# Folding three quarters of the squared channels on VectorE before TensorE's sum for a norm

## What is computed

```python
def rmsnorm(x, g):
    xf = x.astype(jnp.float32)
    var = jnp.mean(xf * xf, axis=-1, keepdims=True)
    return (xf * lax.rsqrt(var + RMS_EPS)).astype(x.dtype) * g

for i in range(DEPTH):                      # first block
    xn = rmsnorm(h, norm_g[i])
    ...
    h = h + jnp.concatenate([y_hg, y_nsa], axis=-1) @ w_out[i]
    gate = jax.nn.sigmoid(rmsnorm(h, ple_norm_g[i]) @ w_pg[i])
    h = h + gate * (p[i] @ w_pp[i])
```

## Time and profile before

| | |
|---|---|
| median of 3 runs | 1159.08 us (1154.74 to 1159.19) |
| the profiled execution | 1159.57 us, its span 1157.7 us |
| TensorE's mean granted clock in it | 0.958 of full speed |
| busy: TensorE, VectorE, ScalarE, GpSimd | 1070.8, 692.2, 583.0, 5.0 us |
| TensorE's weight loads | 1006.8 us |
| read from HBM | 161.43 MB, mean 140 GB/s |
| chain that ended last | TensorE 76%, VectorE 10%, ScalarE 8%, DMA 2% of the span |

### The profile page before, as it was taken

One profiled execution on the slowest core, in us unless ns is written; L12 is line 12 of the kernel. 1 busy time (PEld: TensorE's weight loads), 2 busy tenths in 40 slices (PEclk: granted clock), 3 DMA queues, 4 the chain that ended last, 5 costly groups with the idle time before them and its releaser, 6 DMA issues.

```text
span 1157.7 us, 21354 instructions
## 1 busy us (share of the span) xinstructions
PE 1070.8 (92%) x9033; PEld 1006.8 (87%) x9033; DVE 692.2 (60%) x1020; ACT 583.0 (50%) x830; POOL 5.0 (0%) x13
## 2 busy tenths in 40 slices
PE   3999887898999898999999999999899899999997
PEld 3998776898996776899998999999879789999996
DVE  5556546565547355577665766666544557676664
ACT  4543565466435454565745545545444546545543
POOL 1000000000000000000000000000000000000000
PEclk8999889999999889999999999999998899999998
DMA  8543522253645221274454555555354235555531
GB/s 269 165 130 107 160 74 73 74 166 125 185 116 182 74 74 37 74 254 136 146 166 134 193 182 181 181 183 172 94 173 134 75 109 183 183 181 181 181 109 37
DMA packets 144746, 163.57 MB, mean 141 GB/s; under 512 B 6072, under 2 KB 135552, under 8 KB 144672
## 3 DMA queue, kind: packets, MB, share of 16 engines
q1 hardware_dynamic: 143752, 161.04, 43.3%
q10 hardware_dynamic: 632, 1.30, 0.3%
q0 software_dynamic: 288, 0.14, 0.0%
HBM read 161.43 MB, written 1.05 MB: 140 GB/s over the span
## 4 chain that ended last, share of the span: by engine, by line
PE 76%; DVE 10%; ACT 8%; issue 3%; DMA 2%; SPq 1%; DVEq 0%; ACTq 0%
PE ps L427 23%; PE ps L428 22%; PE ps L429 22%; ACT panels_high L1138 2%; DVE panels_low L1617 2%; PE ps L507 2%; ACT probs L1124 2%; PE ps L443 2%; DMA panels<-in_w_in 1%; DVE neg_max L1640 1%; DVE probs L1656 1%; PE ps L637 1%; PE ps L1031 1%; DMA q_nope<-in_ffn_conv_b 1%; DVE gate_o L2110 1%
## 5 line engine op out<-in xcount | busy, mean ns | idle before, releaser
L427 PE MATMUL ps<-input_high,panels_low 128*128 128x256 f32 x1792 | 525.3, 293 | 36.5 <-DVE input_low L1597 14.2
L428 PE MATMUL ps<-input_low,panels_high 128*128 128x256 f32 x1792 | 516.5, 288 | 0.0
L429 PE MATMUL ps<-input_high,panels_high 128*128 128x256 f32 x1792 | 516.3, 288 | 0.0
L1617 DVE TENSOR_TENSOR panels_low<-panels,panels_high 128x2048 fp32r<-128x2048 f32 (+1 forms) x146 | 330.3, 2265 | 290.7 <-ACT panels_high L1138 283.5
L427 PEld LDWEIGHTS ps<-input_high,panels_low 128*128 128x128 f32 x1792 | 353.6, 197 | 43.8 <-issue 24.9
L428 PEld LDWEIGHTS ps<-input_low,panels_high 128*128 128x128 f32 x1792 | 353.9, 197 | 0.8 <-issue 0.5
L429 PEld LDWEIGHTS ps<-input_high,panels_high 128*128 128x128 f32 x1792 | 353.5, 197 | 0.0
L1138 ACT CAST panels_high<-panels 128x2048 fp32r<-128x2048 f32 (+1 forms) x146 | 274.7, 1883 | 150.8 <-PE ps L429 131.0
L427 PE MATMUL ps<-ffn_hidden_high,panels_low 128*128 128x256 f32 x352 | 100.7, 286 | 3.8 <-DVE ffn_hidden_low L2124 3.8
L428 PE MATMUL ps<-ffn_hidden_low,panels_high 128*128 128x256 f32 x352 | 101.0, 287 | 0.0
L429 PE MATMUL ps<-ffn_hidden_high,panels_high 128*128 128x256 f32 x352 | 100.8, 286 | 0.0
(11 more groups left out here) (274 smaller groups left out, 1065.3 us busy)
## 6 DMA issues: line engine op xcount, KB each, us to landing
panels<-in_ffn_up SPq DMA_DIRECT2D x44, 1024.0 KB, 5.1
panels<-in_w_in SPq DMA_DIRECT2D x32, 1024.0 KB, 5.7
panels<-in_ffn_down SPq DMA_DIRECT2D x22, 1024.0 KB, 5.0
panels<-in_mix_w_in SPq DMA_DIRECT2D x20, 1024.0 KB, 5.3
panels<-in_w_out SPq DMA_DIRECT2D x8, 1024.0 KB, 5.3
panels<-in_w_pg SPq DMA_DIRECT2D x8, 1024.0 KB, 5.2
panels<-in_mix_w_out SPq DMA_DIRECT2D x8, 1024.0 KB, 6.6
panels<-in_w_pp SPq DMA_DIRECT2D x2, 1024.0 KB, 4.9
```

The lines of the kernel that those rows point to most:

```text
L427: pe.matmul(dst, w[1], x[0], start=start, stop=False if not kw else True, **kw)
L428: pe.matmul(dst, w[0], x[1], start=False, stop=False if not kw else True, **kw)
L429: return pe.matmul(dst, w[0], x[0], start=False, stop=stop, **kw)
L1617: V.tensor_tensor(low_slots[slot][:, 0:size], raw[n % SLOTS][:, 0:size], high_slots[slot][:, 0:size].bitcast(F32), ALU.subtract).then_inc( ...
```

## The change

For every norm but the first, VectorE adds squares elementwise in `SQ`, and TensorE sums fewer chunks. For norms 1, 3, 5, 6, 7 and 8, quarters 1 and 2 are added onto quarter 0 (`fold`), so that TensorE sums chunks 0 and 1, where quarter 2 was summed, and chunks 6 and 7: four sums in place of eight. For norms 2 and 4 (`pair_folds`) quarter 1 alone is added onto quarter 0: six sums in place of eight, the first two where quarter 1 was summed. A new semaphore, `sq_folded`, counts the finished folds, and TensorE waits for it. In `add_out` the fold of quarter 1 stands behind the add of quarter 2 of the residual and ahead of `split_after`; the fold of quarter 2 stands ahead of the last add, but behind it for the down products. For norms 2 and 4 the fold stands behind the last add of the update.

```diff
@@ -319,7 +319,8 @@
-        sq_ready = sem("squares_ready")
+        sq_ready, sq_folded = sem("squares_ready"), sem("squares_folded")
+        pair_folds = [2 * l for l in range(1, DEPTH + 1)]
@@ -500,10 +501,17 @@
             def norm_sum(nidx, b=0, quarters=range(4)):
 
                 for g in quarters:
-                    if g == 0:
+                    folded_at = 1 if nidx in pair_folds else 2
+                    if 0 < nidx and g < folded_at:
+                        continue
+                    folded = 0 < nidx and g == folded_at
+                    if g == 0 or folded:
                         begin(f"ms{nidx}", b)
-                    pe.wait_ge(sq_ready, 4 * nidx + g + 1)
-                    for c in (2 * g, 2 * g + 1):
+                    if folded:
+                        pe.wait_ge(sq_folded, nidx)
+                    else:
+                        pe.wait_ge(sq_ready, 4 * nidx + g + 1)
+                    for c in (0, 1) if folded else (2 * g, 2 * g + 1):
                         ins = pe.matmul(ps[b][:, 0:T], ones, sq3[:, c, :], start=(c == 0), stop=(c == ND - 1))
@@ -1657,13 +1665,30 @@
-            def add_out(prefix, suffix=""):
+            def fold(nidx, g):
+
+                dve.wait_ge(sq_ready, 4 * nidx + g + 1)
+                ins = V.tensor_tensor(SQ[:, 0:512], SQ[:, 0:512], SQ[:, g * 512:(g + 1) * 512], ALU.add)
+                if g == 2 or nidx in pair_folds:
+                    ins.then_inc(sq_folded, 1)
+                else:
+                    step(ins)
+
+            def add_out(nidx, prefix, suffix=""):
 
                 for g in range(4):
                     name = f"{prefix}{g}{suffix}"
+                    if g == 3 and prefix != "down":
+                        settle()
+                        fold(nidx, 2)
                     full(dve, name)
                     s = slice(g * 512, (g + 1) * 512)
                     V.tensor_tensor(H[:, s], H[:, s], bank(name)[:, :], ALU.add).then_inc(free(name), 1)
+                    if g == 2:
+                        fold(nidx, 1)
+                    if g == 3 and prefix == "down":
+                        settle()
+                        fold(nidx, 2)
                     if g < 3:
                         split_after(name)
 
@@ -1902,7 +1927,7 @@
-                add_out(f"wo_{l}_")
+                add_out(2 * l + 1, f"wo_{l}_")
@@ -1913,6 +1938,8 @@
                     if g < 3:
                         split_after(f"pg{g}_{l}")
+                    else:
+                        fold(2 * l + 2, 1)
@@ -2077,7 +2104,7 @@
-                add_out(f"wm_{l}_")
+                add_out(nidx, f"wm_{l}_")
@@ -2131,7 +2158,7 @@
-                add_out(f"down", f"_{l}")
+                add_out(nidx, "down", f"_{l}")
```

## The result

The changed kernel takes 1169.14 us in the median of 7 runs (1164.32 to 1171.40) against 1159.08 us of the kernel before: a ratio of 1.0086, with a 95% interval of 1.0064 to 1.0108. It is slower, by 10 us. Timed once more (experiment 9) it had a ratio of 1.0097 (1.0078 to 1.0116). The forecast was 1167.7 us in 1161 to 1172.

The account below looks back on a forecast made before the run. TensorE is busy 92% of the span, but VectorE is already late in norms 1 and 3. 4.30 + 3.12 + 2.30 + 1.60 - 2.65 - 0.55 = +8.1 us on 1159.57 gives 1167.7 us, range 1161 to 1172.

Parts of the forecast that it names:

- Norms 1 and 3, the wait: After the first-block layers' output products: TensorE waits for VectorE's second fold, sums begin 2.15 us later; two norms +4.30 us.
- The signs that were named: 88 sum records, 3.9 us idle in norm 1, fourteen 0.69 us folds, clock under 1, twelve gapless records, unchanged FFN stretches.
- Norms 1 and 3, the clock: Behind the new 3.9 us TensorE idle the granted clock falls once per norm, 1.56 us each: +3.12 us.
- rival (c): Longer stalls: two clock falls each in norms 1 and 3, one each in 6 and 8; about 1174 us, chance 0.07.
- Norms 2 and 4: After the gated update: twelve exposed records behind a later fold, +2.30 us for two; clock fall 0.8 each, +1.60 us.
- Norms 5 and 7: After the mixers' output product, where TensorE sets the pace: four sums go, 1.32 us gained each, -2.65 us for two.
- Norms 6 and 8: After the feed-forward down products: fewer sums but a wait for the second fold; norm 6 -0.55 us, norm 8 0.
- (b): TensorE simply relieved of 28 sums, if quarter 2's fold is ready before bank 3: 1147.5 us, or about 1153; chance 0.05.
- (a): The clock does not fall in norms 1 to 4's new idle pieces, or falls during waits: 1163.0 us, chance 0.24.
- (d): Nothing measurable: later TensorE waits on a weight transfer take up the delay; about 1160 us, chance 0.04.

Follow-up runs that it names:

- experiment 9: The changed kernel timed again unaltered, for a second profile: 1167.84 us, ratio 1.0097 to the kernel before.
- experiment 1: Changed kernel plus four extra 128x512 products on TensorE ahead of the fold wait in norms 1 and 3: 1162.81 us, ratio 1.0049 to the kernel before.
- experiment 2: Kernel before, without folds, but quarter 2's sums of norms 1 and 3 also wait for the last residual add: 1163.39 us, ratio 1.0050.
- (4): Changed kernel with the folded sums of norms 1 and 3 taken behind pp1 instead of ahead of pp0: 1157.77 us, ratio 1.0000 to the kernel before.
- experiments 5: Changed kernel with norms 2 and 4 summed as before, eight sums and no fold: 1164.17 us, ratio 1.0065 to the kernel before.
- experiment 6: Changed kernel with the fold of norms 2 and 4 ahead of the last update instead of behind it: 1163.30 us, ratio 1.0053 to the kernel before.

## Why the prediction was right, and where it was not

**Norms 1 and 3, the wait.** Right, in place, cause and size. The forecast had the fold end at 237.04 and the sums begin at 237.15; they begin at 237.28, in an execution that is 0.1 us late when the norm begins. The bare wait measures +2.18 (experiment 1) and +2.24 (2) for +2.15, and moving the wait takes it away (4). The signs that were named came out as well: 88 records, 4.06 us of idle time for 3.9, fourteen folds of 0.68 us, a clock under 1 behind the wait, twelve records behind norm 2's fold without a gap, and the feed-forward stretches keep their length (to 0.01 us behind norm 5, 0.22 us shorter behind norm 7).

**Norms 1 and 3, the clock.** Right that it falls, too small in size. I took one fall of 1.56 us from the earlier trace rows, with 2 x 1.56 as the upper bound. Measured are 1.77 in the first profile and 2.85 and 3.0 in the second, all inside the bounds. In the five profiles that have the full stall twice the norm costs 3.93 or 3.94 six times and 5.2 to 5.5 four times, of which about 2.2 are the wait; the mean is 4.47, where the forecast has 3.71. The two falls that rival (c) had priced are thus part of the ordinary case.

**Norms 2 and 4.** The exposed sums are right: 1.04 measured for 1.15. The clock on the twelve records is not 0.8 each but nothing or 1.5 to 2.6 (1.04, or 2.57 to 2.73, or 3.67), from one execution to the next. The twelve entries of this code have a mean of 1.93, and the forecast is 1.95. The 0.8 was a middle between two bounds and not a reading, so that it fits the mean is in part luck; no single execution shows it. That both cost something and save nothing is shown by experiments 5 and 6.

**Norms 5 and 7.** -1.50 each for -1.32. The low part, the fold and the add stand back to back on VectorE, and such instructions start 0.60 us apart (620.70, 621.30) though each takes 0.68. I had chained full durations.

**Norms 6 and 8.** Without a fall -0.64 for -0.55, and with the same fall as before -0.13 for 0. Right. In other executions a fall on norm 6 makes it +0.7 to +1.1, which rival (c) had priced and the sum did not. The seven entries of this code have a mean of +0.22 for -0.55 in norm 6 and of -1.11 for 0 in norm 8, the latter because the forecast kept a fall that most of these profiles don't have.

**The rivals.** (b), TensorE simply relieved, was wrong at the point that was named: the fold of quarter 2 is not ready before bank 3 is full. The Trainium skill's page "Perfetto Trace Analysis", section "Identifying the Most-Contended Engine", names the engine of highest occupancy as the one to optimise first. Here that is TensorE, with 92%, and it did lose 9.0 us of busy time; the end moved the other way. (a), no fall of the clock, is excluded by the two profiles of the changed kernel and by experiment 1. (d), nothing measurable, is excluded by the interval, which begins at 1.0064.

**The sum against the profiles.** The changed kernel's first profile is only 4.8 us longer than before's. Its eight norms have 3.93 + 3.93 + 2.08 - 3.00 - 0.64 - 1.27 = +5.0. The second profile is 5.5 us longer, and its norms have +9.2: the attention and mixer stages in between, which no edit touches, take 3.7 us less than in the profile of the kernel before, and their granted clock differs. So no single profile accounts for the 10 us between the medians. The means of the entries above add up to 8.94 + 3.87 - 3.00 + 0.22 - 1.11 = +8.9, against +8.1 forecast and +10 and +11 measured (ratios 1.0086 and 1.0097). That the forecast is so near is partly luck, since errors cancel: it was 1.5 us too low for norms 1 and 3 and 0.8 for norm 6, 1.1 too high for norm 8 and 0.4 for norms 5 and 7. The 1 to 2 us beyond +8.9 are not traced to a place; the entries count from one profile of the kernel before, 1159.57 us, and its medians are 1159.08 and 1156.59.

## What to carry to other kernels

Before work is moved off the busiest engine, look at each place for who is late there: sums that are saved count only where that engine sets the pace (norms 5 and 7). They cost time where their replacement stands behind long work on an engine that is already late (1 and 3), and are worth nothing where they lay in a wait anyway (2 and 4, experiment 6), so that there a fold in the way of the last sums only costs. When a result changes its producer, move its consumer too: here the same folds cost 8 to 11 us with the wait in front of pp0 and gain 1.7 us with it behind pp1 (the two norms' own entries). Price a new idle piece of TensorE together with the dense work behind it, as the clock may fall there.

## What was not expected

The size and the scatter of the clock's part. The same code with the same idle time of 2.02 us went on at the full level once and lost about 1.7 us once (experiment 2), and after a stall of 4.06 to 4.53 us the loss was 1.77 or 2.85 to 3.0 us. So one profile of such a kernel can be 5 us off its median (1164.32 against 1169.14), more than most single edits here are worth; comparing each norm's own duration gave differences that repeat to 0.01 us wherever the clock was the same. And four products that compute nothing, in each of two norms, made the kernel 4 to 5 us faster (experiment 1).
